# Two mixing layers: one stage for the lifts and the head norm, rotary halves added inside the scores, and attention over all heads in one straight line

## The chip, the cores and the metric

The kernel runs on one core of a Trainium2 chip. The metric is the device time of one execution, in microseconds (us); three runs of the kernel before have a median of 6319.23 us. The engines are named as in the profile: PE is TensorE (PEld its weight loads), ACT is ScalarE, DVE is VectorE, POOL is GpSimd, SP is the queue that issues transfers.

## The reference, cut to what matters

A first block (an RWKV branch beside a sparse attention of 8 heads, here `dsa`) is followed by two layers. Each begins with a mixer of two branches over 1024 tokens, and ends with a dense or an expert feed-forward, which the change leaves alone. The mixer:

```python
c_q, c_kv, k_pe, hq, hf, hi, hg = jnp.split(h @ w_in[l], splits, axis=-1)
# _mla, 4 heads
q = (_rmsnorm(c_q, q_a_norm) @ w_q_b)            # 384 -> 4 x (128 + 64)
q_pe = _apply_rope(q_pe, cos, sin); k_pe = _apply_rope(k_pe, cos, sin)
kv = (_rmsnorm(c_kv, kv_a_norm) @ w_kv_b)        # 256 -> 4 x (128 keys + 128 values)
s = einsum('bqhd,bkhd->bhqk', qn, k_nope) + einsum('bqhr,bkr->bhqk', qp, k_pe)
p = softmax(where(key_idx <= q_idx, s, NEG_BIG)); o = p @ v
# _hgrn2, 4 heads, chunks of 64 tokens: a scan over states, then
o = _rmsnorm(o, out_norm) * silu(g_raw)
x = x + concatenate([a, r], axis=-1) @ w_out[l]
```

`_apply_rope` gives two halves, x1 cos - x2 sin and x1 sin + x2 cos. The kernel holds the four products x1 cos, -x2 sin (and so on) in 128 rows, and the sum of rows p and p + 64 is the rotated vector.

## The kernel before, in words

Activations lie transposed, channels in the 128 partitions and 1024 tokens (T) in the free dimension. The program is a line of stages; each is a block with one stream of instructions for each engine and its own semaphores, and ends with a barrier of all engines. Inside a stage an engine does its instructions in the order in which the code writes them. `mix_layer` runs, for each of the two layers, these stages around the change:

- `gated_chunks`: 16 chunks of 64 tokens. PE's loop body `behind` does for chunk n the products (L2121), the turn of the keys (L2131, `turned`), a wait for ACT's copy of them (`k_rows`), the state products (L2138), then `ahead` (L2110), the decay sums of chunk n + 2, and the outputs (L2145, L2146).
- `head_norm_gate`: the head norm of the scan's output `z` and the gate: squares (L2253), column sums over 32 matmuls of one column (L2267), root and reciprocal, spread and turned back (L2258, L2276), products on DVE (L2298, L2296).
- `gemm_t` `up_q`: 8 blocks of 128 queries, plain fp32 matmuls (L293), 3 blocks of the contraction; then `rotate`, 5 blocks multiplied by the rope table on DVE (L1692) and folded from 128 to 64 rows by a matmul with `fold` (L1701); `gemm_t` `up_k`, 4 blocks of keys; and `product_rows` `up_v`, the values, for which both operands are split into a rounded high part and a rest (fp32r), with three matmuls for a product (L1544).
- `attention` `mla`: a loop of PE, ACT and DVE over pairs of heads. Each iteration first copies the pair's queries, rotated queries and values into fixed places in `down` (L1395 on DVE, L1427 on ACT); PE waits for that. Then 16 units (2 heads x 8 blocks of 128 queries) in a skewed line: the scores of unit k (L1364), the transposes of the probabilities of unit k - 2 (L1373), the products with the values of unit k - 3 (L1382). DVE masks and takes the maximum (L1406), scales (L1419); ACT does the exponential (L1439) and two copies (L1435, L1444). At an iteration's end PE waits for the last result to be stored, and only then may the next pair be copied (`drained`). Scores of `mla` are two matmuls that add up: 128 rows of keys, then 64 rows of the rotated part (`turned`).
- `dsa` in the first block is the same function with 8 heads, one matmul for the scores and one copied tensor.

fp32 matmuls appear as two records each in the trace, fp32r ones as one.

## Time and profile before

| | |
|---|---|
| median of 3 runs | 6319.23 us (6315.79 to 6324.01) |
| profiled execution: its time / its span | 6303.05 us / 6301.4 us |
| mean granted clock of TensorE | 0.915 |
| PE busy | 5405.9 us, 86% |
| DVE / ACT / POOL busy | 2798.3 / 2172.3 / 364.6 us |
| DMA | 701.23 MB, mean 111 GB/s |
| costliest stages | the two feed-forwards, from 2140 to 3300 us and from 3870 us on |

The span is the time from the first to the last instruction of one profiled execution; the execution's own time is 1.65 us more. A busy share is an average over stages with different limits, so a stage is read by itself: where it begins and ends, and what the engine that ends it waited for.

### The profile page before, as it was taken

The page shows a single profiled execution, that of the slowest core. Times are in us where ns is not written, and L with a number is a line of the kernel's source. Part 1 is how long each engine was busy: PE and PEld are TensorE (multiplying, and loading weights), DVE is VectorE, ACT ScalarE, POOL GpSimd, SP SyncE. Part 2 cuts the span into 40 slices and gives each one's busy share as a digit, 9 for nine tenths or more (in the row PEclk, how much of TensorE's full clock was granted, in tenths as well). Part 3 has the DMA queues.
Part 4 walks back from the last instruction along what each step waited for, and adds up shares of the span by engine and source line. Part 5 has one row for each costly group of instructions (what it writes and reads, how often), then busy time and mean ns, then how long its engine had stood idle before and what let it go on. Part 6 is the DMA issues. An engine that isn't in the chain of part 4 may idle for free. (4 is left out here: it accounts for less than half of the span.)

```text
span 6301.4 us, 97705 instructions
## 1 busy us (share of the span) xinstructions
PE 5405.9 (86%) x38244; PEld 4596.0 (73%) x38245; DVE 2798.3 (44%) x4351; ACT 2172.3 (34%) x3192; POOL 364.6 (6%) x574
## 2 busy tenths in 40 slices
PE   6964876869888969999798797599999999999994
PEld 5653774657764659999676456598989889898994
DVE  2695332542462345555317233344444445454444
ACT  2212113532333334444333232233333444444432
POOL 0111000000140000000004000100000000000001
PEclk8985997979989979999899888699999999999997
DMA  2110001031000165555210004544444445545544
GB/s 78 39 48 2 2 4 71 0 117 50 24 5 12 54 245 209 197 194 202 85 39 5 17 0 176 179 159 157 157 158 159 174 180 188 185 180 186 185 159 170
DMA packets 110153, 701.23 MB, mean 111 GB/s; under 512 B 12736, under 2 KB 16592, under 8 KB 68560
## 3 DMA queue, kind: packets, MB, share of 16 engines
q1 hardware_dynamic: 95920, 651.24, 28.6%
q0 software_dynamic: 9184, 28.49, 1.3%
q10 hardware_dynamic: 4800, 17.83, 0.7%
q8 instruction: 199, 3.26, 0.2%
q14 instruction: 50, 0.41, 0.0%
HBM read 633.13 MB, written 64.38 MB: 111 GB/s over the span
## 5 line engine op out<-in xcount | busy, mean ns | idle before, releaser
L3075 DVE TENSOR_TENSOR experts_low<-experts_raw,experts_high 128x1024 fp32r<-128x1024 f32 x678 | 810.7, 1224 | 1022.3 <-ACT experts_high L3004 1022.3
L2939 PE MATMUL ps<-experts_xs_high,experts_high 128*128 128x256 f32 (+1 forms) x3584 | 1038.6, 290 | 52.3 <-issue 51.2
L2939 PE MATMUL ps<-experts_xs_low,experts_high 128*128 128x256 f32 (+1 forms) x3584 | 1039.7, 290 | 0.0
L2939 PE MATMUL ps<-experts_xs_high,experts_low 128*128 128x256 f32 (+1 forms) x3584 | 1039.4, 290 | 0.0
L2939 PEld LDWEIGHTS ps<-experts_xs_high,experts_high 128*128 128x128 f32 x3584 | 682.8, 191 | 64.9 <-issue 55.5
L3004 ACT ACTIVATE experts_high<-experts_raw 128x1024 fp32r<-128x1024 f32 x678 | 687.7, 1049 | 63.4 <-DMA experts_raw<-experts 63.4
L2939 PEld LDWEIGHTS ps<-experts_xs_low,experts_high 128*128 128x128 f32 x3584 | 680.3, 190 | 9.4
L2939 PEld LDWEIGHTS ps<-experts_xs_high,experts_low 128*128 128x128 f32 x3584 | 681.2, 190 | 0.0
L2623 PE MATMUL ps<-dense_xs_parts,dense_high 128*128 128x256 f32 x2816 | 499.1, 280 | 4.0 <-DVE dense_xs_parts L2726 2.7
L2623 PEld LDWEIGHTS ps<-dense_xs_parts,dense_high 128*128 128x128 f32 x2816 | 436.5, 189 | 12.3 <-issue 4.8
L2931 PE MATMUL ps<-experts_high,experts_hid_high 128*128 128x512 f32 x1120 | 444.6, 397 | 0.0
L2931 PE MATMUL ps<-experts_low,experts_hid_high 128*128 128x512 f32 x1120 | 442.2, 395 | 0.0
L2623 PE MATMUL ps<-dense_xs_parts,dense_low 128*128 128x256 f32 x1408 | 393.6, 280 | 0.0
L3028 ACT ACTIVATE experts_silu<-ps 128x288 f32<-128x288 f32 (+1 forms) x224 | 89.3, 399 | 832.6 <-PE ps L2939 832.6
L2931 PE MATMUL ps<-experts_high,experts_hid_low 128*128 128x512 f32 x896 | 354.2, 395 | 0.0
L2732 DVE TENSOR_TENSOR dense_low<-dense_raw,dense_high 128x1024 fp32r<-128x1024 f32 x270 | 323.2, 1222 | 64.4 <-ACT dense_high L2661 64.4
L2661 ACT ACTIVATE dense_high<-dense_raw 128x1024 fp32r<-128x1024 f32 x270 | 284.0, 1055 | 54.8 <-PE ps L2608 22.2
L2623 PEld LDWEIGHTS ps<-dense_xs_parts,dense_low 128*128 128x128 f32 x1408 | 265.5, 189 | 0.0
L2931 PEld LDWEIGHTS ps<-experts_high,experts_hid_high 128*128 128x128 f32 x1120 | 210.6, 188 | 39.8
L2931 PEld LDWEIGHTS ps<-experts_low,experts_hid_high 128*128 128x128 f32 x1120 | 210.5, 188 | 39.9
L3034 ACT ACTIVATE experts_hid_high<-experts_hid 128x288 fp32r<-128x288 f32 (+1 forms) x224 | 96.7, 432 | 408.8 <-DVE experts_hid L3093 408.8
L2931 PEld LDWEIGHTS ps<-experts_high,experts_hid_low 128*128 128x128 f32 x896 | 168.2, 188 | 40.7
(530 smaller groups left out, 9262.5 us busy)
## 6 DMA issues: line engine op xcount, KB each, us to landing
experts_raw<-experts SPq DMA_DIRECT2D x226, 1536.0 KB, 6.2
dense_raw<-dense SPq DMA_DIRECT2D x90, 1536.0 KB, 6.7
mixT<-w_in SPq DMA_DIRECT2D x36, 512.0 KB, 3.6
y_slot<-route_blank SPq DMA_DIRECT2D x15, 1152.0 KB, 19.2
out_proj_raw<-w_out SPq DMA_DIRECT2D x48, 256.0 KB, 2.7
proj_keys_raw<-w_in SPq DMA_DIRECT2D x20, 512.0 KB, 3.6
x_mixed<-x_out SPq DMA_DIRECT2D x16, 512.0 KB, 4.7
y_slot<-experts_y ACTq DMA_DIRECT2D x8, 1024.0 KB, 9.2
```

The lines of the kernel that those rows point to most:

```text
L2623: last = nc.tensor.matmul(bank(u, m, SLOTS), w[:, u, m, c], x[:, k, :], start=(k == 0 and i == 0), stop=(k == KD - 1 and i == 2))
L2661: nc.scalar.activation(high[:, v, t, :], raw[:, v, t, :], ACT.Copy).then_inc(rounded, 1)
L2732: nc.vector.tensor_tensor(low[:, v, t, :], raw[:, v, t, :], high[:, v, t, :].bitcast(F32), ALU.subtract).then_inc(split, 1)
L2931: last = nc.tensor.matmul(ps[:, 2 + 2 * a + h, :], x, w[:, v, 2, c], start=first and i == 0, stop=last_one and i == len(terms) - 1)
L2939: last = nc.tensor.matmul(ps[:, m, 0:width], w[:, u, m, c], x[:, k, 0:width], start=(k == 0 and i == 0), stop=(k == KD - 1 and i == 2))
L3004: nc.scalar.activation(high[:, v, t, :], raw[:, v % NR, t, :], ACT.Copy).then_inc(rounded, 1)
L3028: nc.scalar.activation(silu[:, u % 2, 0:width], ps[:, 0, 0:width], ACT.Silu).then_inc(silu_done, 1)
L3034: nc.scalar.activation(hid_high[:, u % 2, 0:width], hid[:, u % 2, 0:width], ACT.Copy).then_inc(hid_rounded, 1)
L3075: nc.vector.tensor_tensor(low[:, v, t, :], raw[:, v % NR, t, :], high[:, v, t, :].bitcast(F32), ALU.subtract).then_inc(split, 1)
```

## The change

The function `lift_and_norm` takes the place of the stages `head_norm_gate`, `up_q`, `rotate`, `up_k` and `up_v`. Keys come first, then queries, then values; all are made with split operands. The four rotary blocks of the queries (units 8 to 11) are multiplied by the rope table on DVE as they leave PSUM, into `down`, and stay 128 rows; the rotary key is multiplied, and folded once into 128 rows whose halves are equal (`fold` becomes 128x128), so that a score product over 128 rows adds the halves. `attention` has no loop, no copies and no `drained`: PE, ACT and DVE get one straight line over all heads. In `gated_chunks`, PE's `ahead` stands before the wait for `k_rows`.

```diff
-                  ("earlier", 128), ("iota8", 8), ("tok", 8), ("pass", NPASS + 1), ("fold", 64), ("spans", 512)):
+                  ("earlier", 128), ("iota8", 8), ("tok", 8), ("pass", NPASS + 1), ("fold", 128), ("spans", 512)):
...
-def attention(core, name, heads, copies, scores, values, masks, scale, outT):
...
-            pe.sem_inc(s["drained"], 1)
-            with pe.Fori(0, heads // 2, 1) as i:
-                pe.wait_ge(s["fetched_a"], (i + 1) * n_copies)
-                pe.wait_ge(s["fetched_v"], (i + 1) * n_copies)
-                core.settle(pe)
-                for k in range(U + 3):
-                    if k < U:
-                        u, b = units[k]
-                        w = (b + 1) * P
-                        if k >= 2:
-                            pe.wait_ge(s["masked"], i * U + k - 1)
...
-                pe.wait_ge(s["stored"], (i + 1) * U)
-                pe.sem_inc(s["drained"], 1)
+            for k in range(U + 3):
+                if k < U:
+                    n, b = units[k]
+                    w = (b + 1) * P
+                    if k >= 2:
+                        pe.wait_ge(s["masked"], k - 1)
...
-                dve.wait_ge(s["drained"], i + 1)
-                core.settle(dve)
-                for dst, src in copies(2 * i + 1, 1):
-                    nc.vector.tensor_copy(dst, src).then_inc(s["fetched_v"], 1)
...
+                    act.wait_ge(s["peak"], k + 1)
+                    if k >= 2:
+                        act.wait_ge(s["turned"], k - 1)
...
+def lift_and_norm(core, name, w_q, w_k, w_v, down, queries, keys, values, key_rope, table, oT, gain, gated, sq):
...
+    units = [(w_k[n], (3, 4)) for n in range(4)] + [(w_q[n], (0, 1, 2)) for n in range(8)]
+    U = len(units)
...
+    rope = down[:, 0:4, :]
...
+    order = (3, 4, 0, 1, 2)
...
+        def _(sp):
+            for n in range(U):
+                if n >= 2:
+                    sp.wait_ge(split, n - 1)
+                sp.dma_start(raw[:, n % 2, 0:size(n)], units[n][0]).then_inc(loaded[n % 2], 16)
+                if n == 3:
+                    sp.dma_start(raw_v[:, :, :], w_v.rearrange("(k p) n -> p k n", p=P)).then_inc(loaded_v, 16)
+        @block.tensor
+        def _(pe):
...
+            for n, (_, blocks) in enumerate(units):
+                pe.wait_ge(split, n + 1)
+                pe.wait_ge(x_split, 2 if n < 4 else 5)
+                if 3 <= n < 11:
+                    pe.wait_ge(freed_a, n - 2)
+                elif n >= 11:
+                    pe.wait_ge(freed_d, n - 10)
+                for k, c in enumerate(blocks):
+                    w = slice(k * P, (k + 1) * P)
+                    for j, (a, x) in enumerate(((high, x_high[:, c, :]), (high, x_low[c]), (low, x_high[:, c, :]))):
+                        for h in range(2):
+                            last = nc.tensor.matmul(core.ps[:, 2 * (n % 3) + h, :], a[:, n % 2, w], x[:, h * HALF:(h + 1) * HALF],
+                                                    start=(k == 0 and j == 0), stop=(k == len(blocks) - 1 and j == 2))
+                last.then_inc(product, 1)
+                if n == 1:
+                    pe.wait_ge(key_scaled, 1)
+                    for h in range(2):
+                        last = nc.tensor.matmul(core.ps[:, 6 + h, :], core.c("fold"), down[:, 5, h * HALF:(h + 1) * HALF],
+                                                start=True, stop=True)
+                    last.then_inc(key_made, 1)
+                if 4 <= n < 8:
+                    j = n - 4
+                    if j == 0:
+                        pe.wait_ge(key_placed, 1)
+                    pe.wait_ge(squared, j + 1)
...
+                    last.then_inc(sums, 1)
+                if n >= 9:
+                    turn(n - 9)
+            pe.wait_ge(v_split, 2)
+            for b in range(NT):
+                if b < 6:
+                    pe.wait_ge(freed_d, b // 2 + 2)
+                else:
+                    pe.wait_ge(v_placed, b - 5)
...
+                last.then_inc(v_made, 1)
+                if b == 3:
+                    turn(3)
+        @block.scalar
+        def _(act):
+            copy = nc.scalar.activation
+            def round_unit(n):
+                act.wait_ge(loaded[n % 2], 16 * (n // 2 + 1))
+                if n >= 2:
+                    act.wait_ge(product, n - 1)
+                copy(high[:, n % 2, 0:size(n)], raw[:, n % 2, 0:size(n)], ACT.Copy).then_inc(rounded, 1)
+            round_unit(0)
+            for m, c in enumerate(order):
+                copy(x_high[:, c, :], down[:, c, :], ACT.Copy).then_inc(x_rounded, 1)
+                if m == 1:
+                    round_unit(1)
+            for n in range(U):
+                if n + 2 < U:
+                    round_unit(n + 2)
+                if n < 8:
+                    act.wait_ge(product, n + 1)
+                    copy(keys[:, n, :] if n < 4 else queries[:, n - 4, :], two(2 * (n % 3)), ACT.Copy).then_inc(freed_a, 1)
+                if n == 2:
+                    act.wait_ge(key_made, 1)
+                    copy(key_rope, two(6), ACT.Copy).then_inc(key_placed, 1)
+                if 2 <= n < 6:
+                    copy(sq[:, n - 2, :], oT[:, n - 2, :], ACT.Square).then_inc(squared, 1)
+                if n in (6, 7):
+                    act.wait_ge(loaded_v, 16)
+                    copy(high_v[:, n - 6, :], raw_v[:, n - 6, :], ACT.Copy).then_inc(v_rounded, 1)
+                if n == 8:
+                    act.wait_ge(meansq, 1)
+                    copy(stat[:, 1, :], stat[:, 0, :], ACT.Sqrt).then_inc(rooted, 1)
+                    act.wait_ge(inverse, 1)
+                    for j in range(2):
+                        copy(spread[j], stat[:, 2, j * NT:(j + 1) * NT].unsqueeze(2).to_broadcast([P, NT, P]), ACT.Copy)\
+                            .then_inc(spreaded, 1)
...
+            for b in range(NT):
+                act.wait_ge(v_made, b + 1)
+                copy(values[:, b, :], core.ps[:, b % 6, :], ACT.Copy).then_inc(v_placed, 1)
         @block.vector
         def _(dve):
...
+            def split_unit(n):
+                dve.wait_ge(rounded, n + 1)
...
+                tt(low[part], raw[part], high[part].bitcast(F32), ALU.subtract).then_inc(split, 1)
+            def norm(j):
+                dve.wait_ge(turned, j + 1)
...
+                nc.vector.scalar_tensor_tensor(gated[:, j, :], gated[:, j, :], gain, two(6), ALU.mult, ALU.mult).then_inc(normed, 1)
+            split_unit(0)
+            for m, c in enumerate(order):
+                dve.wait_ge(x_rounded, m + 1)
+                tt(x_low[c], down[:, c, :], x_high[:, c, :].bitcast(F32), ALU.subtract).then_inc(x_split, 1)
+                if m == 1:
+                    split_unit(1)
+            tt(down[:, 5, :], down[:, 5, :], table[:, :], ALU.mult).then_inc(key_scaled, 1)
+            for n in range(U):
+                if n + 2 < U:
+                    split_unit(n + 2)
+                if 1 <= n < 5:
+                    tt(gated[:, n - 1, :], gated[:, n - 1, :], oT[:, n - 1, :], ALU.mult).then_inc(gated_done, 1)
+                if n in (6, 7):
+                    dve.wait_ge(v_rounded, n - 5)
+                    tt(low_v[:, n - 6, :], raw_v[:, n - 6, :], high_v[:, n - 6, :].bitcast(F32), ALU.subtract).then_inc(v_split, 1)
+                if n == 8:
+                    dve.wait_ge(sums, 4)
+                    nc.vector.tensor_scalar(stat[:, 0, :], core.ps[:, 6, 0:4 * NT], 1.0 / P, 1e-6, ALU.mult, ALU.add).then_inc(meansq, 1)
+                    dve.wait_ge(rooted, 1)
+                    nc.vector.reciprocal(stat[:, 2, :], stat[:, 1, :]).then_inc(inverse, 1)
+                if n >= 10:
+                    norm(n - 10)
+                if n >= 8:
+                    dve.wait_ge(product, n + 1)
+                    tt(rope[:, n - 8, :], two(2 * (n % 3)), table[:, :], ALU.mult).then_inc(freed_d, 1)
+            norm(2)
+            norm(3)
...
                 last.then_inc(s["turned"], 1)
+                if sums:
+                    ahead(n + 2, u, i + 1)
                 pe.wait_ge(s["k_rows"], n + 1)
...
                 for h in range(H):
                     mm(ps[:, 7, h * P:(h + 1) * P], kt[:, h % 2, :], value[:, u, h * P:(h + 1) * P], start=True, stop=True)
-                if sums:
-                    ahead(n + 2, u, i + 1)
...
+        z = sb("z", [P, 4, T])
...
-            head_norm_gate(core, f"gated_norm{l}", z[:, :, :], core.v(f"hgn{l}", 0), mixT[:, 4:8, :])
         with ExitStack() as s2:
             sb2 = lambda name, shape: s2.enter_context(nc.sbuf_tensor(f"{name}{l}", shape, F32))
...
             values = sb2("values", [P, NT, HALF])
...
-            gemm_t(core, f"up_q{l}", d[f"w_q{l}"], 8, 3, down, lambda n: at(queries, n))
-            rotate(core, f"rotate{l}", [queries[:, 4 + j, :] for j in range(4)] + [down[:, 5, :]], table, turned)
-            gemm_t(core, f"up_k{l}", d[f"w_k{l}"], 4, 2, down[:, 3:5], lambda n: at(keys, n))
-            product_rows(core, f"up_v{l}", down[:, 3:5, :], 2, d[f"w_v{l}"], 1, values)
...
+            key_rope = sb2("key_rope", [P, T])
+            lift_and_norm(core, f"lift{l}", d[f"w_q{l}"], d[f"w_k{l}"], d[f"w_v{l}"], down, queries, keys, values, key_rope[:, :], table,
+                          z, core.v(f"hgn{l}", 0), mixT[:, 4:8, :], mixT[:, 0:4, :])
             attention(core, f"mla{l}", 4,
-                      lambda n, u: [(qbuf[:, u, :], at(nope, n)), (rbuf[:, u, :], at(turned, n)),
-                                    (vbuf[:, u, :, :], values[:, :, bass.ds(n * P, P)])],
-                      lambda u, b, n: [(qbuf[:, u, b * P:(b + 1) * P], at(keys, n)),
-                                       (rbuf[:, u, b * P:(b + 1) * P], turned[:, 4, :])],
-                      lambda u, j: vbuf[:, u, j, :],
+                      lambda n, b: [(queries[:, n, b * P:(b + 1) * P], keys[:, n, :]),
+                                    (down[:, n, b * P:(b + 1) * P], key_rope[:, :])],
+                      lambda n, j: values[:, j, n * P:(n + 1) * P],
...
-        attention(core, "dsa", 8, lambda n, u: [(qbuf[:, u, :], at(q_abs, n))],
-                  lambda u, b, n: [(qbuf[:, u, b * P:(b + 1) * P], down[:, 2, :])],
-                  lambda u, j: latent[:, j, :],
+        attention(core, "dsa", 8, lambda n, b: [(q_abs[:, n, b * P:(b + 1) * P], down[:, 2, :])],
+                  lambda n, j: latent[:, j, :],
...
-    put("fold", (p % 64) == n)
+    put("fold", (p % 64) == (np.arange(P)[None] % 64))
```

PE in the loop of `gated_chunks`, one chunk, before (gated_decays is the operand of `ahead`, gated_kt the turned keys in SBUF):

```order
L2121 MATMUL ps<-gated_qs,gated_ks 64x64 x28
L2131 MATMUL ps<-cst,gated_ks 64x128 x4
L2134 REGISTER_ALU
L2135 REGISTER_ALU
L2138 MATMUL ps<-gated_value,gated_kt 128x128 x4
L2103 ISA
L2110 MATMUL ps<-cst,gated_decays 128x512 x4
```

and the same place now:

```order
L2252 MATMUL ps<-gated_qs,gated_ks 64x64 x28
L2262 MATMUL ps<-cst,gated_ks 64x128 x4
L2234 ISA
L2241 MATMUL ps<-cst,gated_decays 128x512 x4
L2267 REGISTER_ALU
L2268 REGISTER_ALU
L2271 MATMUL ps<-gated_value,gated_kt 128x128 x4
```

The four wide matmuls of `ahead` moved from behind the state products to between the turn and them.

ACT in the new stage, from the copy of the last query block that it evacuates to the values (mixT is `sq`, the room of the squares and of the spread reciprocals):

```order
L1765 ACTIVATE lift_high<-lift_raw 128x384
L1777 ACTIVATE queries<-ps 128x1024
L1785 ACTIVATE lift_high_v<-lift_raw_v 128x512
L1765 ACTIVATE lift_high<-lift_raw 128x384
L1788 ACT_TABLE_LOAD
L1788 ACTIVATE lift_stat<-lift_stat 128x32
L1791 ACTIVATE mixT<-lift_stat 128x1024 x2
L1765 ACTIVATE lift_high<-lift_raw 128x384
L1795 ACTIVATE mixT<-lift_stat 128x1024 x2
L1799 ACTIVATE values<-ps 128x512 x8
```

The root and the spreads of the head norm, which had a stage of their own, stand between the roundings of the weights of units 10 and 11; all four heads share one root.

## Rows read from the trace of the kernel before

**Rows 1.** By stretch: length, busy PE, PEld, DVE, ACT, POOL (count), clock, DMA, GB/s

```profile
1845.20:1976.30 131.10, 103.48 (x292) 59.25 (x292) 27.86 (x36) 34.88 (x38) 0.00 (x0) 0.81 0.07 20
3489.30:3624.40 135.10, 106.35 (x293) 60.01 (x293) 27.86 (x36) 34.88 (x38) 0.00 (x0) 0.80 0.07 20
1976.30:2121.80 145.50, 138.67 (x624) 78.93 (x624) 50.51 (x163) 58.96 (x132) 0.00 (x0) 0.92 0.00 0
3624.40:3782.40 158.00, 151.18 (x624) 84.61 (x624) 50.41 (x163) 58.68 (x132) 0.00 (x0) 0.84 0.00 0
...
3705.00:3725.00 20.00, 20.00 (x36) 8.22 (x36) 5.43 (x23) 4.93 (x15) 0.00 (x0) 0.50 0.00 0
...
1963.00:1970.00 7.00, 6.99 (x31) 5.44 (x29) 4.73 (x7) 0.00 (x0) 0.00 (x0) 1.00 0.00 0
```

**Rows 2.** Timeline of PE, head norm to keys; start, length [idle before <-releaser]

```profile
1846.34 6.99 PE L2267 MATMUL ps<-cst,gated_norm_sq 128*128 128x1 f32 x32 [3.18 <-ACT gated_norm_sq L2253]
1853.19 1.95 PE L2276 MATMUL ps<-cst,gated_norm_sq 128*128 128x128 f32 x8
...
1871.83 43.56 PE L293 MATMUL ps<-down,up_q_w 128*128 128x512 f32 x96 [4.69 <-DMA up_q_w<-w_q]
...
1918.54 7.08 PE L1701 MATMUL ps<-queries,cst 128*64 128x512 f32 x16 [3.15 <-DVE queries L1692]
...
1931.66 16.90 PE L293 MATMUL ps<-down,up_k_w 128*128 128x512 f32 x32 [4.32 <-DMA up_k_w<-w_k]
```

**Rows 3.** Timeline of the start of the values' stage, all engines

```profile
1950.38 0.80 SPq L1523 DMA_DIRECT2D up_v_raw<-w_v  x2
...
1956.57 0.79 PE L1544 MATMUL ps<-up_v_high,up_v_x_high 128*128 128x512 f32 x1 [8.01 <-DVE up_v_low L1571]
```

**Rows 4.** Timeline where the attention of the first layer begins

```profile
1971.78 1.28 ACT L1427 ACT_TABLE_LOAD   x1 [15.66 <-PEq L1348]
...
1973.08 1.06 ACT L1427 ACTIVATE down<-queries 128x1024 f32 x1
...
1976.33 0.79 PE L1364 MATMUL ps<-keys,down 128*128 x2 [6.34 <-ACT down L1427]
```

**Rows 5.** Timeline of DVE: the widest mask of each of the four heads, first layer

```profile
2004.57 1.23 DVE L1406 CUSTOM_DVE_ANT_0 mla_masked<-ps,cst 128x1024 f32<-128x1024 f32 x1 [3.60 <-PE ps L1364]
...
2036.37 1.23 DVE L1406 CUSTOM_DVE_ANT_0 mla_masked<-ps,cst 128x1024 f32<-128x1024 f32 x1 [3.60 <-PE ps L1364]
...
2080.78 1.23 DVE L1406 CUSTOM_DVE_ANT_0 mla_masked<-ps,cst 128x1024 f32<-128x1024 f32 x1 [3.60 <-PE ps L1364]
...
2112.58 1.23 DVE L1406 CUSTOM_DVE_ANT_0 mla_masked<-ps,cst 128x1024 f32<-128x1024 f32 x1 [3.60 <-PE ps L1364]
```

**Rows 6.** Timeline of PE inside the scores of a wide block, first layer

```profile
2001.12 1.12 PE L1364 MATMUL ps<-turned,down 64*128 64x512 f32 x2
2002.18 1.12 PE L1364 MATMUL ps<-keys,down 128*128 x2
```

**Rows 7.** Timeline of the first block's attention: PE's start, widest masks of heads 2, 3, 4, 6

```profile
1058.06 2.33 PE L1364 MATMUL ps<-down,queries 128*128 128x128 f32 x5 [5.12 <-ACT queries L1427]
...
1093.93 1.22 DVE L1406 CUSTOM_DVE_ANT_0 dsa_masked<-ps,masks 128x1024 f32<-128x1024 f32 x1 [1.14 <-PE ps L1364]
...
1119.45 1.23 DVE L1406 CUSTOM_DVE_ANT_0 dsa_masked<-ps,masks 128x1024 f32<-128x1024 f32 x1 [1.15 <-PE ps L1364]
...
1140.28 1.23 DVE L1406 CUSTOM_DVE_ANT_0 dsa_masked<-ps,masks 128x1024 f32<-128x1024 f32 x1 [1.14 <-PE ps L1364]
...
1187.39 1.22 DVE L1406 CUSTOM_DVE_ANT_0 dsa_masked<-ps,masks 128x1024 f32<-128x1024 f32 x1 [1.15 <-PE ps L1364]
```

**Rows 8.** Timeline of one chunk of the scan, first layer: PE, DVE, POOL

```profile
1759.60 1.13 PE L2138 MATMUL ps<-gated_value,gated_kt 128*128 128x128 f32 x8 [0.77 <-ACT gated_kt L2177]
...
1758.52 1.09 DVE L2194 TENSOR_TENSOR gated_prod<-ps,cst 128x896 f32<-128x896 f32 x1 [0.76 <-PE ps L2121]
...
1757.94 0.19 POOL L2075 COPY gated_ends<-gated_span 128x4 f32<-128x4 f32 x1 [1.31 <-DVE gated_state L2218]
```

271 lines of the change are left out of this document (107 added, 164 removed).

## The prediction

> **What bounds the kernel now.** I read first the busy time by stretch, to see what the touched stages are worth. From the first work of the head norm to the first score of `mla` it is 131.1 us in the first layer and 135.1 in the second; from there to the last stored output it is 145.5 and 158.0 us [rows 1]. PE is busy for most of each, so the question is what PE does and in which gaps it stands still. Other engines are far from full: DVE 27.9 and ACT 34.9 of 131.1 us.
>
> Next the timeline of PE, for the gaps. In the head norm PE does 64 column sums and transposes at low clock; then each stage begins with a barrier, a weight transfer and a wait of 3 to 5 us [rows 2]. The query matmuls take 43.56 us for 96 records. The fold shows what a record costs at full clock: 16 in 7.08 us, less 0.6 for the last one's own length, is 0.43 us each, so 0.86 for a 512-column fp32 matmul of two records. An fp32r matmul of the same width is one record, and 31 of them fill 7.0 us: 0.226 each, at granted clock 1.00 [rows 1].
>
> Third, `mla`. The widest masks of heads 1 and 2 lie 31.80 us apart; heads 2 and 3, which an iteration's end separates, lie 44.41 us apart [rows 5]. So a seam costs 12.6 us. At the start PE waits 6.34 us, for three copies on ACT behind a table load [rows 4]. After a seam the clock is low for long: 0.50 from 3705 to 3725 us, with PE busy all the time [rows 1]. And in the scores a pair of records of 64 or 128 rows takes 1.05 us where the two alternate [rows 6], against the 0.86 above: each alternation loses 0.19 us.
>
> Last, the scan and `dsa`. In a chunk PE waits 0.77 us for the turned keys, while DVE has a wait of 0.76 us for PE and POOL one of 1.31 [rows 8]. In `dsa` a head takes 20.83 us inside an iteration (1119.45 to 1140.28) and 25.52 over a seam (1093.93 to 1119.45) [rows 7].
>
> **The new stage, a term for each thing PE does in a layer.**
> - Start. The values' stage did the same: transfer, rounding, rest, first matmul, 6.2 us from issue to PE [rows 3]. Here two blocks of the activations must be split before PE starts, where before it was one of them and one of the weights, which is half as wide: I take 6.4 us.
> - Keys and queries: 4 units of 12 and 8 of 18 fp32r matmuls, 192 x 0.226 = 43.4 us. Before, 64 fp32 ones took 55 us at full clock.
> - Values: 48 x 0.226 = 10.8 us, as before.
> - Low clock at the start: the query stage took 43.56 us where 96 x 0.43 = 41.2, so a cold start costs 2.4 us [rows 2]. It is paid once, where the stages before paid it for each.
> - Rotary key fold: 2 x 0.86 = 1.7 us. The four folds of the queries go.
> - Column sums and transposes of the head norm: 32 in 6.99 us and 8 in 1.95 at low clock, so half at full clock: 3.5 and 3.9 us [rows 2].
> - End: 0.4 us for the last matmul's length, 0.6 for ACT's copy of it, and an estimate of 1.2 for the barrier to the first score.
>
> Sum 74.3 us; I add 0.3 for hand-overs: 74.6. This holds if nothing but PE sets the pace. An ACT copy of 1024 columns takes 1.06 us [rows 4] and a DVE pass about 1.2 (the 1.23 of [rows 5]). In a query unit of 4.1 us ACT has a rounding of 384 columns, a copy and a square, some 2.6 us, and DVE at most two passes and a short one; both fit. The tight place is unit 8, where ACT does the next rounding, table load (1.28), root and two spreads (2.1) with DVE's reciprocal between: some 4 us after unit 8 ends until the first spread is there, against the 4.1 us of unit 9 that cover it. In the tail DVE has for each of units 9 to 11 a product with the table and a norm, 2.5 of 5.1 us. The transfers are small and two units ahead. Saved: 131.1 - 74.6 = 56.5 and 135.1 - 74.6 = 60.5, **117 us**. The copies before the first score are in this.
>
> **mla.** Without alternation a head loses 24 x 0.19 = 4.6 us: 31.8 becomes 27.2. The other bound comes from `dsa`, whose head takes 20.83 with one matmul for a score; a second one of the same columns (4608, nine times 512) adds 9 x 0.86 = 7.7: 28.5. I take 27.7, nearer to the first, because `dsa` has idle time of PE that a second matmul fills in part. The first head up to its widest mask took 28.2 us (1976.33 to 2004.57), and the mean clock of 0.92 puts 23 of the 145.5 us at 1.2 GHz [rows 1], of which I give 9 to this start and the rest to the seam; less 4.5 for these and 4 for the alternation it is about 20. The tail from the last widest mask to the last output is 9.2 us (2112.58 to 2121.8) [rows 1, 5]. So 20 + 3 x 27.7 + 9.2 = 112.3 us for each layer, against 145.5 and 158.0: **78.9 us**. The clock's part rests on this: in the rows a wait of 3.15 us before the fold left PE at full speed, one of 4.32 us before the keys was followed by low clock (16.90 us for 32 records, 13.8 at full) [rows 2]; the new gap before the scores is 2 to 2.5 us.
>
> By the row, the side of 128 rows is as slow as the side of 64 where they alternate [rows 6], and neither is where the rows stay the same. The Trainium skill (TensorE: Matmul & The Clock Gate, The mechanism) says that a weight load overlaps running matmuls only when its row group differs; by that rule the wide operand would lay its load bare just as now, the widening would bring nothing, and the sum would be 203 us. Another page of the Trainium skill (TensorEngine Tiling (Array Packing), Key Properties) says that a change of tiling mode drains the engine, by which it is the alternation that costs, and the sum stays. The first rule is the third rival below.
>
> **dsa.** Three seams. The first costs 4.7 us (25.52 - 20.83); the second, with a head more, lies between 1140.28 and 1187.39, 47.11 - 2 x 20.83 = 5.5 us; the third as the second: 15.7 us [rows 7]. PE's wait of 5.12 us before the first score [rows 7] shrinks by ACT's table load and copy, 2.4 us; the clock then stays up, an estimate of 0.8 us. **19 us**. ACT's added wait for `turned` before the exponential costs nothing: ACT has waited for the same value just before, for the copy of the transposes.
>
> **The scan.** PE's wait of 0.77 us in a chunk is covered by the 2 us of `ahead`. What `ahead` needs, the decays of chunk n + 2 and the exponential of n + 1, is there some 2 us earlier. The chunk gets shorter by about 0.75 us; next in line are DVE, with 0.76 us of wait before the masks, and POOL, with 1.31. 14 chunks in each of two layers, 28 x 0.75 = **21 us**. The bounds are 0 and 21.6; as the waits of the others are about as wide or wider, I take the upper one.
>
> `fold` in the first block is a slice of a wider constant: nothing, the same bytes are read. `z` lives longer: nothing.
>
> **Sum.** 117 + 79 + 19 + 21 = 236 us. Against the profiled execution, 6303.05 us, this gives 6067. The median of the runs lies 16.2 us above that execution, so I forecast **6083 us**.
>
> **Rivals.**
> 1. The scan gains nothing, because DVE or POOL takes over. For it: DVE's wait is hardly wider than what is to be gained. Against: DVE has to follow PE, so its wait shrinks no further than PE's own work allows. 6104 us.
> 2. The new stage is not paced by PE: two or three hand-overs of 3 to 5 us each are bare (the root, the spreads, the rotary products that free PSUM for units 11 and the values). For it: 24 semaphores in a skewed line written by hand. 10 us a layer: 6103 us; with rival 1 6124.
> 3. Widening brings nothing, since a load of 128 rows after 128 rows lies as bare as one after 64: 8 heads x 4.1 = 33 us less gained: 6116 us. Against: in the second half of the values' stage PE is busy 6.99 of 7.00 us and PEld 5.44 of it, all with 128 rows [rows 1]: the loads lie under the matmuls.
> 4. Low clock persists where the stretches now join, as it did for 20 us and more after a seam at full load [rows 1]: half of 30 us in each attention, 6113 us.
> 5. Slower than before: TensorE is granted 1.2 GHz through the merged stretches. PE's full-clock time there is 66 us in a stage and 110 in an attention, 352 us in all, so the low level throughout adds 352 us and gives 6435. It decides against the change from two thirds of these stretches on (236 us). Against: both attentions come back to full clock after their seams and have means of 0.92 and 0.84 with them [rows 1]. The supply of instructions for the unrolled line would show in the same way; in the loop's first pass, whose instructions are new, a head took the same 31.80 us as in the second [rows 5].
> 6. That the change doesn't do what it says: a copy or a drain that stays. The code has none left.
>
> **Numbers.** The forecast 0.70; rivals 1 and 2 0.19 together, 3 0.05, 4 0.04, 5 and unknown ones 0.02. The range takes in 1 to 4 and their pairs, up to 6135; downwards, 27.2 us for a head (4 us less), a shorter stage and the runs' own scatter of 8 us give 6055. What a measurement of this kernel can tell from no change is about 0.2%, 13 us; all cases but the last are far beyond it. Faster 0.98, same 0.01, slower 0.01.
>
> **What would show it.** The new stage should be 74 to 77 us from its first work to the first score, with PE's waits inside under 1 us and the clock up from about 5 us on. A head of `mla` should take 27 to 28.5 us at every seam, one of `dsa` 20.8 at each of seven. Pairs of records in the scores should be 0.86 us apart. A chunk should be 0.75 us shorter, and PE's wait for the turned keys be gone. A clock of 0.50 in the first 15 us of `mla`, a wait of PE for spreads or for DVE's rotary products, or a chunk as long as before would each prove a part wrong; together they could make 6130.

## The result and the profile after

The changed kernel takes 6044.01 us (median of 4 runs, 6036.01 to 6047.35), the kernel before 6317.51 (4 runs, 6312.17 to 6324.01): a ratio of 0.9565, interval 0.9548 to 0.9581. The forecast was 6083 us, range 6055 to 6135. The sign and the mechanism held; the time lies 11 us below the range. The profiled execution of the changed kernel took 6045.13 us, its span 6043.5.

The table cuts three executions at starts that their traces have in common: `dsa` from the first product with `uk` to the first with `uv`; the scan from its first decay sum to its last state update; from there to the first mask of `mla`; `mla` from that mask to the last product with the values; the experts from their first product with `xs_high` to the last. The middle column is a second execution of the kernel before, made later (first experiment). Both layers are added up.

| us | before | before, again | changed | saved | forecast |
|---|---|---|---|---|---|
| `dsa` and its start | 201.5 | 202.3 | 178.2 | 23.3 | 19 |
| scans | 275.6 | 274.1 | 248.2 | 27.4 | 21 |
| head norm and lifts | 272.0 | 273.8 | 158.5 | 113.5 | 117 |
| `mla` | 298.7 | 308.1 | 221.8 | 76.9 | 79 |
| experts | 2167.8 | 2175.9 | 2154.2 | 13.6 | 0 |
| everything else | 3085.9 | 3090.6 | 3082.7 | 3.2 | 0 |

The four touched rows saved 241.1 us where 236 were forecast. (The forecast cut two of them at other places, at the first and the last work of a stage; cut there, the head norm and the lifts saved 111.5 us and `mla` 78.9.) (The dense feed-forward, in the last row, runs from 2276 to 3037 us in the trace of before and not to 3300: the second layer's projections follow.) What made the result better than the range is in the difference of the first two columns and in the experts' row, neither of which the sum had.

By stretch in the changed kernel, as [rows 1]: the new stage in both layers, from its first transfer to the first score, and both attentions. Columns: stretch, length, busy PE, PEld, DVE, ACT, POOL (count), clock, DMA share, GB/s.

```profile
1804.50:1881.90 77.40, 69.99 (x340) 58.10 (x340) 28.86 (x34) 33.50 (x46) 0.00 (x0) 0.93 0.12 35
3347.90:3425.20 77.30, 69.70 (x340) 57.87 (x341) 28.86 (x34) 33.51 (x47) 0.00 (x0) 0.93 0.11 35
1881.90:1994.20 112.30, 111.09 (x624) 80.89 (x624) 48.70 (x160) 55.75 (x129) 0.00 (x0) 1.00 0.00 1
3425.20:3537.50 112.30, 111.08 (x624) 80.89 (x624) 48.70 (x160) 55.74 (x129) 0.00 (x0) 1.00 0.00 1
```

The new stage is 77.4 us; PE is busy 70.0 of them, and 5.97 are its start and 1.51 its end, so inside it PE waits for nobody. An attention (first score to last output) is 112.3 us at a clock of 1.00, to the tenth what the sum had (20 + 3 x 27.7 + 9.2 = 112.3).

PE in the new stage: start, a group of column sums, a group of transposes, the end of the values, the first scores. SPq is the queue that issues the transfers.

```profile
1804.47 0.80 SPq L1697 DMA_DIRECT2D lift_raw<-w_k  x2
...
1810.44 0.77 PE L1722 MATMUL ps<-lift_x_high,lift_high 128*128 128x512 f32 x1 [7.93 <-DVE lift_x_low L1818]
...
1829.88 1.84 PE L1737 MATMUL ps<-cst,mixT 128*128 128x1 f32 x16
1831.58 0.72 PE L1722 MATMUL ps<-lift_x_high,lift_high 128*128 128x512 f32 x2
...
1857.67 1.03 PE L1708 MATMUL ps<-cst,mixT 128*128 128x128 f32 x8
1858.46 0.71 PE L1722 MATMUL ps<-lift_x_high,lift_high 128*128 128x512 f32 x2
...
1880.05 0.39 PE L1751 MATMUL ps<-lift_high_v,lift_x_low 128*128 128x512 f32 x1
1881.95 0.46 PE L1356 MATMUL ps<-keys,queries 128*128 128x128 f32 x2 [1.51 <-PEq L117]
```

Transposes of a head take 0.79 us (1857.67 to 1858.46), 3.2 for four. The sums of a head take 1.70 us (1829.88 to 1831.58), 6.8 for four: twice the term in the sum. The gap before the scores is 1.51 us.

The scores of a wide block in the changed kernel, which answer to [rows 6]: the starts of pairs are 0.86, 0.85, 0.86 us apart.

```profile
1898.01 1.02 PE L1356 MATMUL ps<-keys,queries 128*128 128x512 f32 x2
1898.87 1.02 PE L1356 MATMUL ps<-key_rope,down 128*128 128x512 f32 x2
1899.72 1.02 PE L1356 MATMUL ps<-keys,queries 128*128 128x512 f32 x2
1900.58 1.02 PE L1356 MATMUL ps<-key_rope,down 128*128 128x512 f32 x2
```

The widest masks on DVE, as [rows 5] and [rows 7]: two heads of `mla` in the second layer, two of `dsa`.

```profile
3472.70 1.23 DVE L1388 CUSTOM_DVE_ANT_0 mla_masked<-ps,cst 128x1024 f32<-128x1024 f32 x1 [2.86 <-PE ps L1356]
3500.50 1.22 DVE L1388 CUSTOM_DVE_ANT_0 mla_masked<-ps,cst 128x1024 f32<-128x1024 f32 x1 [2.86 <-PE ps L1356]
...
1107.01 1.22 DVE L1388 CUSTOM_DVE_ANT_0 dsa_masked<-ps,masks 128x1024 f32<-128x1024 f32 x1 [1.15 <-PE ps L1356]
1127.47 1.22 DVE L1388 CUSTOM_DVE_ANT_0 dsa_masked<-ps,masks 128x1024 f32<-128x1024 f32 x1 [1.15 <-PE ps L1356]
```

A head of `mla` takes 27.8 us (27.79 or 27.80 at all six distances; forecast 27.7), one of `dsa` 20.47 at all seven, where the forecast had left the 20.83 of the loop. A narrow block of `dsa`, from the start of its score to its mask, first in the second execution of the kernel before, then in the changed kernel:

```profile
1129.13 0.60 PE L1364 MATMUL ps<-down,queries 128*128 128x256 f32 x2
1129.95 0.42 DVE L1406 CUSTOM_DVE_ANT_0 dsa_masked<-ps,cst 128x256 f32<-128x256 f32 x1 [1.57 <-PE ps L1364]
```

```profile
1111.43 0.60 PE L1356 MATMUL ps<-down,q_abs 128*128 128x256 f32 x2
1112.07 0.42 DVE L1388 CUSTOM_DVE_ANT_0 dsa_masked<-ps,cst 128x256 f32<-128x256 f32 x1 [1.38 <-PE ps L1356]
```

PE in one chunk of the changed scan, which answers to [rows 8], and behind it the same work in a chunk before:

```profile
1727.67 0.61 PE L2262 MATMUL ps<-cst,gated_ks 128*64 128x128 f32 x8
1728.20 1.99 PE L2241 MATMUL ps<-cst,gated_decays 64*128 64x512 f32 x8
1730.12 1.16 PE L2271 MATMUL ps<-gated_value,gated_kt 128*128 128x128 f32 x8
1731.12 0.33 PE L2276 MATMUL ps<-gated_qs,gated_state 128*128 128x64 f32 x2
1731.29 0.39 PE L2277 MATMUL ps<-gated_attn,gated_value 128*128 128x64 f32 x2
```

```profile
1750.25 0.61 PE L2131 MATMUL ps<-cst,gated_ks 128*64 128x128 f32 x8
1751.63 1.13 PE L2138 MATMUL ps<-gated_value,gated_kt 128*128 128x128 f32 x8 [0.77 <-ACT gated_kt L2177]
1752.69 1.99 PE L2110 MATMUL ps<-cst,gated_decays 64*128 64x512 f32 x8
1754.61 0.43 PE L2145 MATMUL ps<-gated_qs,gated_state 128*128 128x64 f32 x2
1754.88 0.39 PE L2146 MATMUL ps<-gated_attn,gated_value 128*128 128x64 f32 x2
```

The wait for the turned keys is gone and no other took its place. From one chunk's state products to the next chunk's it is 6.96 and 7.03 us in turn (6.96 and 7.12 in the second layer), where it was 7.96.

### The profile page after: what moved, and what is told of

Its sections match the earlier page's. It is cut to its first block and busy times, and to the rows that moved or that the text cites. A ratio compares the mean times of both kernels' runs of the same rounds, so it can differ in the third digit from the quotient of the medians.

```text
span 6043.5 us, 97005 instructions
## 1 busy us (share of the span) xinstructions
PE 5253.8 (87%) x38340; PEld 4585.2 (76%) x38341; DVE 2798.2 (46%) x4337; ACT 2154.0 (36%) x3195; POOL 363.1 (6%) x574
## 6 DMA issues: line engine op xcount, KB each, us to landing
y_slot<-route_blank SPq DMA_DIRECT2D x15, 1152.0 KB, 19.7
```

## The experiments

**The kernel before, once more.** No edit.

> The kernel before, profiled once more, to see what one execution differs from another. The stages that the change touches saved 241 us between the two traces, the profiled executions 258 and the medians 273.5, so 17 to 32 us lie in stages whose code is the same; 13.6 of them lie in the experts' matmuls (2167.5 us against 2153.9), where PE stood still before an expert's first matmul 7 times for 6 to 10 us before and 3 or 8 us after. Theory A: these starts are a matter of the execution; then this trace has another mix of them, a length of the experts' stage between 2150 and 2185 us, and all touched stages within 0.5 us of the first trace. Theory B: they belong to the program (where its instructions lie); then the experts take 2167.5 us again, within 2 us, with the same waits.

It took 6326.45 us, 23 more than the first profiled execution of the same kernel. The experts took 2175.9 us, 8 more, with the same group of waits (below). What neither theory had asked about is `mla` in the first layer: 152.6 us from first mask to last product where the first trace has 143.1. The traces with the scan's edit and with 128 counting instructions (below) have 152.6 and 152.5, the one with 64 of them 145.9 and 152.9 in its two executions. The clock tells them apart. By stretch from the first mask on, this execution:

```profile
1982.40:1992.40 10.00, 10.00 (x16) 3.54 (x17) 2.94 (x14) 2.08 (x7) 0.00 (x0) 0.50 0.00 0
1992.40:2002.40 10.00, 10.00 (x21) 4.43 (x20) 2.49 (x10) 2.85 (x8) 0.00 (x0) 0.50 0.00 0
2002.40:2012.40 10.00, 10.00 (x25) 4.45 (x23) 1.75 (x5) 1.68 (x4) 0.00 (x0) 0.64 0.00 0
2012.40:2022.40 10.00, 10.00 (x59) 6.73 (x59) 5.46 (x15) 5.05 (x10) 0.00 (x0) 1.00 0.01 2
```

and the first profiled one:

```profile
1978.00:1988.00 10.00, 10.00 (x20) 3.52 (x21) 3.79 (x18) 2.87 (x9) 0.00 (x0) 0.63 0.00 0
1988.00:1998.00 10.00, 10.00 (x38) 4.76 (x39) 3.38 (x11) 3.94 (x11) 0.00 (x0) 1.00 0.00 0
```

Behind PE's wait of 6 us, and counted from the first mask on, the clock is at 0.50 (1.2 GHz) for 27 us in one and for 7 in the other, and that is the 9.5 us of `mla`. The execution on which the sum was made was a lucky one (the shortest first `mla` of the six traces that have the loop), in a stretch that the change removes: `mla` took 110.9 us in both layers of all six traces of the changed kernel and of its early-start variants.

**The scan's edit alone**, on the kernel before.

```diff
                 last.then_inc(s["turned"], 1)
+                if sums:
+                    ahead(n + 2, u, i + 1)
                 pe.wait_ge(s["k_rows"], n + 1)
...
-                if sums:
-                    ahead(n + 2, u, i + 1)
```

> The kernel before with the one edit in the scan: PE's sums of chunk n + 2 ahead of its wait for the turned keys. Theory A (the prediction's, with the size that the trace of the changed kernel shows): a chunk takes 7.0 us instead of 7.96 in both layers, the scans together 27.5 us less, 0.4% of the time (ratio 0.9956). Theory B (the shorter chunk of the changed kernel needs the rest of the change, for instance what is placed where in memory): a chunk stays at 7.96, or goes to 7.2 as predicted, ratio 0.9967 to 1. Nothing else moves: dsa's head 20.83, mla's 31.80.

6287.93 us (6 runs) against 6310.33: ratio 0.9958, interval 0.9946 to 0.9971. A chunk takes 6.96 to 7.12 us behind the first two (the last two apart), the scans 123.5 and 124.0 us instead of the 137.0 and 137.1 of the second execution before. Theory A. So the 27 us of the table are this edit's own, and the first rival of the prediction is out.

**The line alone**, on the kernel before, with the rotated part at 64 rows and the old stages ahead.

```diff
-            attention(core, f"mla{l}", 4,
-                      lambda n, u: [(qbuf[:, u, :], at(nope, n)), (rbuf[:, u, :], at(turned, n)),
...
+            attention(core, f"mla{l}", 4,
+                      lambda n, b: [(queries[:, n, b * P:(b + 1) * P], keys[:, n, :]),
+                                    (turned[:, n, b * P:(b + 1) * P], turned[:, 4, :])],
+                      lambda n, j: values[:, j, n * P:(n + 1) * P],
```

> The kernel before with the new attention alone: one line over all heads, no copies, but the rotated part still 64 rows and the stages ahead as before. Theory A (a score of 64 rows after one of 128 loses time; the line only takes the seams away): a head of mla takes 31.8 us at every seam; 23 us less in dsa, 17 and 30 in the two layers, about 70 us in all (ratio 0.989). Theory B (the width is worth nothing; the shorter head comes from the line and its plain operands): a head takes 27.8 us and 102 us go (ratio 0.984). In both dsa's head takes 20.47 us at all seven distances, as in the changed kernel, if that size comes with the line.

6196.29 us (5 runs): ratio 0.9817, interval 0.9803 to 0.9830. Heads of `mla` 31.80 us at all six distances, of `dsa` 20.47 at all seven:

```profile
2000.04 1.22 DVE L1388 CUSTOM_DVE_ANT_0 mla_masked<-ps,cst 128x1024 f32<-128x1024 f32 x1 [3.60 <-PE ps L1356]
2031.84 1.22 DVE L1388 CUSTOM_DVE_ANT_0 mla_masked<-ps,cst 128x1024 f32<-128x1024 f32 x1 [3.60 <-PE ps L1356]
```

Theory A for the head: the line takes the seams, the width does the rest. But 114 us went, not 70. Against the second execution of the kernel before, `dsa` gave 23, the two `mla` 25.6 and 28.6, the starts of the two attentions (PE no longer waits for three copies) 6 and 8, and the experts 28. From the last state update to the first mask it is 129.7 and 130.2 us here and 79.3 and 79.2 in the changed kernel: the merged stage is worth 101 us by itself.

**Three ways to cut the rows.** All on the changed kernel. Half of each rotary sum is left out in the first two, and half of the keys' part too in the third, so only their attention is compared (the routing of tokens, and with it the experts' work, differs).

```diff
-                                    (down[:, n, b * P:(b + 1) * P], key_rope[:, :])],
+                                    (down[0:64, n, b * P:(b + 1) * P], key_rope[0:64, :])],
```

> The changed kernel, with only the first 64 of the 128 rows of the rotary operands read in the scores; half of each rotary sum is left out. Theory A (rows of 64 and 128 in turn lose 0.19 us at each change): a head of mla takes 31.8 us again, 4.0 more, 32 us for the 8 heads (ratio to the kernel before 0.962). Theory B (the width is worth nothing): 27.8 us and the time of the changed kernel (0.9565). The other stages stay as in the changed kernel.

31.80 us at all six distances: theory A. The expected time of the whole was missed, for the reason just given: 6334.75 us (6 runs), a ratio of 1.0033 instead of 0.962, as the experts take 2400.8 us with the other routing. The second also swaps the loops over operands and column halves:

```diff
-                    for c in range(0, w, HALF):
-                        e = min(w, c + HALF)
-                        for m, (q, keys) in enumerate(ops):
+                    for m, (q, keys) in enumerate(ops):
+                        for c in range(0, w, HALF):
+                            e = min(w, c + HALF)
```

> The changed kernel with 64 rows of the rotary operands read (half of each rotary sum is left out), and in a score both column halves of the keys' part first, then both of the rotary part. In wide blocks the rows change twice a unit instead of four times, in narrow ones twice as before: 16 changes a head instead of 24. Theory A (a change of rows costs 0.17 us, from 4.0 us for 24 of them in the run with 64 rows): a head of mla takes 27.79 + 16 x 0.17 = 30.5 us. Theory C (each narrow load costs, whatever stands before it): the narrow loads are as many as before, so 31.8 us.

The third reads `queries[0:64, ...]` and `keys[0:64, ...]` as well.

> The changed kernel with only 64 rows read of all score operands (half of each sum is left out): keys and rotary part both 64 rows, transposes and products with the values 128 as ever. Theory A (changes cost): 2 changes a unit, 16 a head, 30.5 us. Theory C (narrow loads cost 0.33 us each time, 4.0 us over 12 matmuls): twice as many narrow matmuls, 27.79 + 8.0 = 35.8 us. Theory D, the rule by which a load is hidden only behind a matmul of another group of rows: it would make this head the slowest of all, and the one of 128 rows slower than that of 64 and 128 in turn, which the changed kernel already speaks against.

The widest masks of two heads in the run with 64 rows, then in the one with the loops swapped, then in the one with 64 rows everywhere:

```profile
1943.14 1.22 DVE L1388 CUSTOM_DVE_ANT_0 mla_masked<-ps,cst 128x1024 f32<-128x1024 f32 x1 [3.60 <-PE ps L1356]
1974.94 1.22 DVE L1388 CUSTOM_DVE_ANT_0 mla_masked<-ps,cst 128x1024 f32<-128x1024 f32 x1 [3.60 <-PE ps L1356]
```

```profile
1946.13 1.23 DVE L1388 CUSTOM_DVE_ANT_0 mla_masked<-ps,cst 128x1024 f32<-128x1024 f32 x1 [3.21 <-PE ps L1356]
1976.37 1.23 DVE L1388 CUSTOM_DVE_ANT_0 mla_masked<-ps,cst 128x1024 f32<-128x1024 f32 x1 [3.21 <-PE ps L1356]
```

```profile
1954.43 1.23 DVE L1388 CUSTOM_DVE_ANT_0 mla_masked<-ps,cst 128x1024 f32<-128x1024 f32 x1 [3.20 <-PE ps L1356]
1984.65 1.23 DVE L1388 CUSTOM_DVE_ANT_0 mla_masked<-ps,cst 128x1024 f32<-128x1024 f32 x1 [3.20 <-PE ps L1356]
```

31.80, 30.24 and 30.22 us, against 27.79 with 128 rows everywhere. Two kernels with different operands but 16 changes of rows a head each take the same time though one has twice as many narrow matmuls, and the one with 24 changes takes more: theory A, at (31.80 - 27.79) / 24 = 0.167 and (30.22 - 27.79) / 16 = 0.152 us a change. That the rule of the Trainium skill on hidden loads (TensorE: Matmul & The Clock Gate, The mechanism) would cost the widened kernel its gain, as the third rival had it, is refuted for this pattern; the other page's (TensorEngine Tiling (Array Packing), Key Properties), that a change of mode drains the engine, agrees with these numbers.

**A wait before the first score.** The changed kernel with idle copies on ACT, for which PE waits.

```diff
+            for i in range(held):
+                nc.scalar.activation((masked_s, probsT)[i // 2][:, i % 2, :], core.c("causal")[:, 0:T], ACT.Copy).then_inc(s["held"], 1)
```

> The changed kernel with four idle copies of 1024 columns on ACT at the start of each mla attention, for which PE waits: a wait of about 6 us before the first score instead of 1.5. From first score to widest mask of the first head it is 18.9 us in the changed kernel (its first score's mask at 1882.7, the widest at 1901.6). Theory A (the gap itself costs the clock): a granted clock of 0.50 behind it for 10 us or more, and 24 to 28 us to the widest mask, in both layers. Rival (the clock fell in the kernel before for another reason, the thin work of the stages ahead): 19 us and a clock of 1.00. Heads 2 to 4 27.8 us in either case.

PE waited 5.44 us. From the first score on, by stretch:

```profile
1892.50:1899.50 7.00, 7.00 (x17) 4.42 (x18) 2.54 (x13) 3.33 (x8) 0.00 (x0) 0.62 0.00 0
1899.50:1914.50 15.00, 15.00 (x67) 9.39 (x66) 6.58 (x20) 6.72 (x16) 0.00 (x0) 1.00 0.00 1
```

The clock fell, so the wait does it, but it was back soon: the stretch at 0.50 is 6.9 us long, and first mask to widest mask takes 21.0 and 20.8 us in the two layers instead of 19.0, not the 24 to 28 expected. So here the gap alone costs 2 us beside itself. In the kernel before, whose scores of 64 and 128 rows in turn follow a gap of 6.3 us, the stretch at 0.50 was 10 and 31 us long in the first layer of its two executions and 24 in the second layer of both; that the rows make the difference is not shown. All three kernels with cut rows start their first attention behind the same 1.51 us as the changed one and still show 0.50 in it, for 30 us in the one with 64 rows everywhere (1890 to 1920), while PE's records leave no gap; the line alone, with rows in turn, kept 1.00. Why one execution falls and another doesn't stays open.

**Counting instructions ahead of the experts.** They do nothing but move PE's later instructions, and stand where PE waits 58 us for a gather.

```diff
+            for _ in range(64):
+                core.settle(pe)
             pe.wait_ge(gathered, 48)
```

> The kernel before, with 64 counting instructions on PE ahead of the experts' matmuls, where PE waits 58 us for the first gather anyway: they only move PE's later instructions. In three traces with the loop in attention (the kernel before twice, the one with the scan's edit) PE waits 8 to 10 us before the first matmul of the experts 5, 6 and 7, and the stage takes 2168 to 2176 us; in the two of the same data with the straight line it waits 3 us there and the stage takes 2148 and 2154. Theory B (where the instructions lie decides): the waits change as a group, to 3 us or to other values, and the stage takes about 2150 for at least one of 64, 128 and 192 instructions. Theory E (something else of the straight line, as the time at which the stage begins or what memory holds): 2168 to 2176 us and 9 us again.

> As the run with 64 counting instructions on PE ahead of the experts' matmuls, with 128. Theory B: a stage of about 2150 us with waits of 3 us for one of the shifts of 64, 128 and 192. Theory E: 2168 to 2176 us.

> The kernel before with 64 counting instructions on PE ahead of the experts' matmuls, timed against the kernel before. In one execution each, 64 and 128 of them brought the experts' stage from 2168 to 2176 us down to 2146 and 2150. Theory B (where PE's instructions lie decides, so it is a matter of the program): the median falls by 20 to 30 us as well (ratio 0.995 to 0.997, 1 outside the interval), and the trace shows 2146 us again within 3 us. Theory F (it was these executions' luck): ratio 1 within 0.001, and the stage anywhere between 2145 and 2176 us.

On the kernel before the experts took 2145.9 us with 64 and 2149.8 with 128, and 2150.1 in the second execution with 64 (4 us from the first, where 3 were expected at most); timed, 6292.51 us (6 runs) against 6312.25, ratio 0.9966, interval 0.9954 to 0.9979. 64 instructions that do nothing make the kernel 20 us faster. PE before its first matmul for the sixth expert, in the second execution of the kernel before, the one with 64 instructions, and the changed kernel:

```profile
5453.27 0.55 PE L2939 MATMUL ps<-experts_xs_high,experts_high 128*128 128x256 f32 x1 [9.68 <-issue]
```

```profile
5436.60 0.55 PE L2941 MATMUL ps<-experts_xs_high,experts_high 128*128 128x256 f32 x1 [3.16 <-issue]
```

```profile
5180.62 0.35 PE L3001 MATMUL ps<-experts_xs_high,experts_high 128*128 128x256 f32 x1 [2.97 <-issue]
```

"issue" means that nothing the profile shows held PE; ACT and DVE had their results ready. Ahead of experts 5, 6 and 7 PE waits 8 to 10 us in both traces of the kernel before and in the scan's edit, and 3 us in all with padding here, in the line alone and in the changed kernel; ahead of experts 2 to 4 it waits 5 to 10 us in every one of these traces. The stage is a loop with branches, so PE jumps back for each expert. The Trainium skill (Runtime: NRT & Kernel Launch, Instruction fetch mechanics) says that instructions come in blocks of 16 KiB and that a taken branch to a place outside what is held stalls for a fetch; the waits and their answer to padding agree with it, though no fetch was looked at in a trace.

**The start of the new stage earlier**, with and without such instructions.

```diff
-            round_unit(0)
             for m, c in enumerate(order):
                 copy(x_high[:, c, :], down[:, c, :], ACT.Copy).then_inc(x_rounded, 1)
-                if m == 1:
-                    round_unit(1)
+                if m < 2:
+                    round_unit(m)
```

(DVE's splits in the same order; PE's first unit waits for one block, then for the second.)

> The changed kernel with another order at the start of the new stage: ACT rounds and DVE splits the first block of activations while the first weights are still under way, and PE starts on one block instead of two. The stage now issues its first transfer at 1804.47 and PE starts at 1810.44, 5.97 us later. If ACT's copy of 1.06, the rounding and split of the weights (0.4 each) and DVE's 1.2 are the whole chain, PE starts 3.0 to 3.5 us after the first issue, and the stage takes 2.5 to 3 us less in each layer. Rival: the second unit's weights or the second block come too late, PE waits there instead, and less than 1 us is gained. Either is too small for the time of one execution.

> The changed kernel with the earlier start of the new stage alone, timed. In its trace the stage is 3.2 and 3.1 us shorter in the two layers and nothing else moved, so its median should be 6.3 us below the changed kernel's 6044.0: 6038, ratio to the kernel before 0.9562 or so, which a few runs can hardly tell from 0.9565. The experts' stage again 2150 to 2154 us (theory B). If it is a matter of the execution (theory F), the stage may be anywhere from 2143 to 2176.

> The changed kernel with the earlier start and 64 counting instructions on PE ahead of the experts' matmuls. The start gives 5 to 6 us. In the changed kernel PE waits 7.8 to 8.3 us before the experts 2 to 4 and 3 us before 5 to 7, in 2154 us. Theory B says only that the waits move as groups: the stage may come to anything between 2140 and 2180 us. So 6015 to 6065 us; below 6030 it would be a version that beats the changed kernel.

> The same with 128 counting instructions on PE ahead of the experts' matmuls. Unpadded the experts' stage took 2150 us, with 64 instructions 2175. If the place of PE's instructions decides and 16 KB of them (256) are a period, one of 0, 64, 128 and 192 is bad on the kernel with the straight line, as 0 was the bad one of 0, 64 and 128 on the kernel before: 2143 to 2155 us here. If every instruction added on PE there costs, it would be above 2175 us.

> The same with 192 counting instructions. Theory B, one bad place in four: 2143 to 2155 us. If every added instruction costs: above 2175 us, and more than with 128.

Without padding PE started 2.81 us after the first transfer's issue in the timed kernel's trace (1809.88 to 1812.69), and the stage was 3.1 to 4.0 us shorter in each layer. Timed it took 6035.07 us (5 runs, 6028.51 to 6037.54), ratio 0.9556, interval 0.9543 to 0.9569; 9 us below the changed kernel, with intervals that overlap, so the gain is shown by the trace and likely, not shown, by the time. The experts: 2150.0 and 2147.3 without, 2175.3 with 64, 2145.9 with 128, 2152.5 with 192. With 64 it was timed too: 6063.83 us (5 runs), ratio 0.9600, interval 0.9586 to 0.9615, slower than without. PE before the sixth expert with 64, then with 128:

```profile
5186.62 0.55 PE L3003 MATMUL ps<-experts_xs_high,experts_high 128*128 128x256 f32 x1 [9.65 <-issue]
```

```profile
5167.43 0.46 PE L3003 MATMUL ps<-experts_xs_high,experts_high 128*128 128x256 f32 x1 [3.38 <-issue]
```

So it is place and not number: one of the four places tried is bad here, and the kernel before stood on a bad one of the three tried there. The straight line and the new stage put more instructions on PE ahead of the experts than the loops and stages that they replace; the line alone already moved the experts' loop to where PE waits 3 us.

## Why the prediction was right and where it was wrong

- **Bound and mechanism: right.** PE paced all touched stages, and no wait took the place of those removed.
- **The new stage: 77.4 us, forecast 74.6.** The mis-sized term is the column sums. [Rows 2] show 32 records in 6.99 us and a group of transposes behind it, and I took the 32 for all; there are 64 a layer, and at full clock they cost 6.8 us, not 3.5. The transposes cost 3.2 (forecast 3.9), the start 5.97 (6.4), the end 1.9 from the last matmul's start (2.2); the remaining 0.9 us is low clock and hand-overs.
- **mla: right**, 27.8 a head and 112.3 a layer (19.7 + 3 x 27.8 + 9.2 where the sum had 20 + 3 x 27.7 + 9.2). That the head came out to 0.1 us is partly luck: 27.7 was picked between 27.2 and 28.5. The reading of [rows 6], that the change of rows costs and not the narrowness, is what the three cuts and the line alone confirm. The term took 0.19 us a change from one place; over a head it is 0.152 to 0.167, so 24 changes are 4.0 us and not 4.6.
- **dsa: 23.3, forecast 19.** 2.9 us are 8 x (20.83 - 20.47), which I had as zero. In the loop DVE has a counting instruction between its wait and the mask. From the start of a 256-column score to its mask it is 0.82 us in the second execution of the kernel before (1129.13 to 1129.95) and 0.64 in the changed one (1111.43 to 1112.07), and PE waits on this chain in narrow blocks: of a head PE is busy 20.17 of 20.83 us before and 20.15 of 20.47 now. The operands and the waits changed together with the counting instruction, and no run took it out alone, so that it is the cause is likely and not shown.
- **The scan: 27.4, forecast 21.** A chunk gains 0.97, not 0.75, and the 21.6 us taken as the upper bound was none: it counted PE's wait as all that a chunk can lose. 0.77 is PE's wait. Up to 0.1 comes from the outputs: their first pair takes 0.17 us (1731.12 to 1731.29) where the trace of before has 0.27 (1754.61 to 1754.88). The state products take 1.00 us until the next instruction instead of 1.06, and the turn 0.53 instead of 0.61 without the wait. All three come with another neighbour in front or behind; which property of it counts was not tried.
- **The touched stages together: 241, forecast 236.** That they come so near is in part errors that cancel: the lifts gave 5.5 us less than forecast, the scan 6 and `dsa` 4 more.
- **The step that failed** is the last one: "The median of the runs lies 16.2 us above that execution, so I forecast **6083 us**". It took the distance for something that the change can't touch. Of the 23 us between the two executions of the kernel before, 9.4 lie in `mla` and 8.1 in the experts; the change removed the first, and the experts got shorter with it. The changed kernel's profiled execution lies 1.1 us above its median (6045.13 and 6044.01), so nothing was to be added. The 16.2 us also rested on three runs: later series of the kernel before have medians of 6310 (13 runs), 6312 (10) and 6315 us (9), 7 to 12 above that execution.
- **The omission** is that stages with unchanged code were taken as unchanged. The experts are 13.6 us shorter than in the first execution and 21.7 shorter than in the second, and padding alone moves them by as much.
- **The 39 us missed:** 16.2 for the distance and 1.1 for where the changed kernel's own execution lies; the other 22 are the distance of that execution from the sum's 6067: 13.6 in the experts, 5 in the touched stages, 3.2 everywhere else, which is within what two executions of one kernel differ by (4.7).
- **The rivals:** the first fell with the scan's edit alone, the second with PE's 0 us of wait inside the stage, the third with the cuts, the fourth and fifth with a clock of 1.00 in both attentions.

## What to carry to other kernels

Before a profiled execution's distance to the median is added to a forecast, find the stage in which two executions differ: if the change touches it, the distance goes with it. On TensorE, count changes in the number of rows between neighbouring matmuls; operands doubled or left unfolded to 128 rows can be cheaper than exact ones of 64, as they were here by 4.0 us in a head. And before 0.3% is credited to an edit, look at the waits in loops behind it, and time the kernel with a few dozen instructions that do nothing on the same engine.

## What the runs showed of the hardware that was not expected

- 64 idle instructions on PE move a later loop with branches by 20 to 29 us, either way: 6312 to 6293 us on the kernel before, 6035 to 6064 on the early start.
- A change between 64 and 128 rows from one fp32 matmul to the next costs 0.152 to 0.167 us in the heads of `mla`; 64 rows cost nothing more by themselves.
- The granted clock fell to 0.50 and stayed there for 30 us with no gap in PE's records, in a kernel whose scores use 64 rows; behind a gap of 5.44 us with 128 rows throughout it was back after 7. Each is one execution, and the line alone, with 64 rows in it, kept 1.00.
- From a narrow score of `dsa` to its mask it is 0.82 us in the loop and 0.64 in the straight line; a counting instruction between DVE's wait and the mask is the likely cause, not isolated.
